# Latent attention of a two-block transformer kernel: one written order per engine over eleven lines of work, four banks in one ring

## The chip, the cores and the metric

The kernel runs on one core of one Trainium2 chip. The metric is the device time of one execution in microseconds (us), lower is better. Of the kernel before, three runs are shown: 2634.11, 2634.42 and 2637.79 us.

## What is computed

Two transformer blocks follow each other on 512 tokens of width 1024. The first (dilated attention with retention, cross attention, a gated MLP) is untouched here. The second has a gated delta-rule branch and a latent-attention branch over the same tokens and 256 context tokens, a merge of the two by gates, and an MLP. The change lies between the end of the delta rule and the merge, and that stage computes:

```python
q = (_rms(cq, q_a_norm) @ w_uq).reshape(B, T, 8, 192)
kv = (_rms(ckv, kv_a_norm) @ w_ukv).reshape(B, T, 8, 256)
k_nope, v = kv[..., :128], kv[..., 128:]
k = concatenate([k_nope, broadcast(k_rope)])
q, k = _rms(q, q_norm), _rms(k, k_norm)        # then rotary on the last 64
s = einsum('bqhd,bkhd->bhqk', q, k) * 192 ** -0.5
o = softmax(s) @ v                             # 512 queries, 768 keys
y = _rms(o_gdn, w_norm) * silu(z)              # the delta rule's output, gated
```

cq, ckv, k_rope and z are projections of the normed tokens (ckv and k_rope of the context too).

## The kernel before

Everything is held with channels on partitions. Large projections are made from weight chunks of 128 x 1024, streamed by SyncE's DMAs into raw slots (three in turn in this stage). ACT writes the rounded chunk (`hi_to`), DVE the remainder (`lo_to`), and `project` makes three rounded products for each of eight input tiles: 24 products of 128 x 512 for a chunk. Attention itself is in exact f32.

Each engine runs one instruction queue in order. Between engines there are semaphores by name: `up` counts an event, `at` waits for it, `fence` for several. A PSUM bank may be written again when the events in `free[bank]` have come. The functions are generators: each `yield` ends a turn, and the order in which a driver calls the generators of an engine is the order of its queue.

The latent stage has these parts, each with one generator per engine it uses:

- **Ranks** (`rank_pe`, `rank_act`, `rank_dve`): cq by three chunks, ckv by two, k_rope by one; sums of squares by a product with ones, root, scaling. They run whole, before all else.
- **Front of a head** (`front_pe`, L2257, and its ACT, DVE and POOL parts): queries from cq (on even heads a second product for the rotary parts of two heads), keys and values from ckv; squares by ACT, the rotary part's squares added by POOL, sums by TensorE, roots by ACT, scaling by DVE. The squares of queries and of both key groups (512 and 256 tokens) share two buffers in turn, `SQM`, L2168.
- **Attention of a head** (`latent_pe`, L2417): four blocks of 128 queries. A score block is four products into a pair of banks, 2 and 3 or 4 and 5 in turn; DVE takes the row maximum, ACT the exponential with its sum, DVE scales by the reciprocal, TensorE transposes six squares of 128 into two banks, DVE copies the four of the first and ACT the two of the second. After the fourth block the six value products run. `attend_turns2`, L2412, is the written order of the 12 turns within a head.
- **Gates and norm** (`z_pe`, L2111, and others): eight projections of z with a Silu each, then for eight groups the norm of the delta rule's output (POOL squares, DVE sums, ACT root, DVE scaling), a transposition and the multiplication with the gate.

`latent_step`, L2506, puts these together on every engine: in step h it calls in turn the attention of head h-1, the front of head h and four turns of the gates and norm, one turn each, until all are at their end. `weave` is that round-robin:

```python
for step in range(9):
    latent_step(step, lambda h: latent_pe(e, h), lambda h: front_pe(e, h, take), zg)

def latent_step(step, attend, front, zg):
    weave(*(([attend(step - 1)] if step else []) + ([front(step)] if step < 8 else []) + [some(zg, 4)]))
```

So steps 0 to 3 hold two gate projections each, steps 4 to 7 two groups of norm turns. TensorE's front and gates take banks 0 and 1 in turn (`take`, L2530), the transposes and the values 6 and 7. A Silu and an exponential are in different ACT table sets, and a switch is an extra instruction (L140). SyncE (`latent_sp`, L2509) loads w_uq, w_uk and w_uv head by head into one place each, so each load waits for the products of the head before; the gate chunks stand between them, and the first merge chunks behind all. The delta-rule stage before this one already takes its order from strings, one letter per turn (`walk_streams`, L2029).

Lines that the rows name are those of helpers: L130 product, L133 transpose, L142 activation, L143 exponential with sum, L140 table load, L146 copy, L155 tensor-tensor, L160 tensor-scalar, L163 scalar-tensor-tensor, L172 row reduction.

Of the kernel before, what the change touches and what calls it, by code (L numbers as in the profile page):

```python
# [16 lines left out]
KT = 8  # L17
# [186 lines left out]
def program(nc, D, out):  # L204
    tally = Tally()
    at, up, land = tally.at, tally.up, tally.land
    with ExitStack() as ctx:
# [1821 lines left out]
        def walk_streams(engine, streams):  # L2029

            for x in TURNS[engine]:
                next(streams[x], None)
            for g in streams.values():
                whole(g)
# [6 lines left out]
        def gdn_pe(e):  # L2041
# [6 lines left out]
            walk_streams("PE", dict(  # L2048
# [4 lines left out]
        def gdn_act(e, got):  # L2053
            fence(e, mlp_end)
            walk_streams("ACT", dict(
# [4 lines left out]
        def gdn_dve(e, got):  # L2060
            walk_streams("DVE", dict(
# [4 lines left out]
        def gdn_pool(e):  # L2066
            fence(e, mlp_end)
            walk_streams("POOL", dict(
# [18 lines left out]
        KR2, SQR = hcT, hcT + 768  # L2087
# [12 lines left out]
        chunks[first_merge + 5]["after"] = [("l_uq", 7), ("l_uk", 7)]  # L2100

        def z_turns():
            for mt in range(8):
                yield "z", mt, 0
                yield "z", mt, 1
            for blk in range(4):
                for g in range(2):
                    yield "norm", blk, g
                    yield "turn", blk, g

        def z_pe(e, take):  # L2111
            for what, i, g in z_turns():
                if what == "z" and g == 0:
                    b = take()
                    whole(project(e, CI["w_z", i], KT, [(b, NT, *HX, hx)]))
                    free[b], BK["z", i] = [("z_ev", i)], b
                elif what == "turn":
                    b = take()
                    fence(e, [("z_on", i, g)] + free[b])
                    for j in range(4):  # L2120
                        t = e.transpose(P(b * 512 + j * 128, 128), S(OS + i * 1024 + g * 512 + j * 128, 128), IDN)
                    t.then_inc(*up("z_tr", i, g))
                    free[b], BK["z_tr", i, g] = [("z_y", i, g)], b
                yield

        def z_act(e, got):
            for what, i, g in z_turns():
                if what == "z" and g == 0:
                    hi_to(e, got, min(CI["w_z", i][0] + 1, last_two))
                    e.wait_ge(*at("w_used", CI["w_z", i][0]))  # L2130
                    e.act(S(y1 + i * NT, NT), P(BK["z", i] * 512, NT), ACT.Silu).then_inc(*up("z_ev", i))
                elif what == "norm":
                    e.wait_ge(*at("z_red", i, g))
                    e.act(S(ST8 + 8, 4), S(ST8, 4), ACT.Ln, scale=1.0 / 128, bias=S(EPS6, 1)).then_inc(*up("z_ln", i, g))
                    e.wait_ge(*at("z_ln", i, g))
                    e.act(S(ST8 + 16, 4), S(ST8 + 8, 4), ACT.Exp, scale=-0.5).then_inc(*up("z_rs", i, g))
                yield

        def z_dve(e, got):
            for what, i, g in z_turns():  # L2140
                og = OS + i * 1024 + g * 512
                if what == "z" and g == 0:
                    lo_to(e, got, min(CI["w_z", i][0] + 1, last_two))
                elif what == "norm":
# [11 lines left out]
        def z_pool(e, before):  # L2156
            for what, i, g in z_turns():
                if what == "norm":
                    if i or g:
                        e.wait_ge(*at("z_red", i - 1 + g, 1 - g))  # L2160
# [37 lines left out]
        def rank_act(e, got):  # L2198
# [4 lines left out]
            for k in range(3):  # L2203
                square_of(e, k, cqT + k * NT, NT, [("cq_ev", k)])
# [803 lines left out]
```

## Time and profile before

| | before |
|---|---|
| median of three runs | 2634.42 us |
| the profiled execution's own time | 2637.32 us |
| span of its trace | 2635.5 us |
| TensorE busy, whole span | 2431.4 us, 92% |
| DVE, ACT, POOL busy | 48%, 37%, 10% |
| mean granted TensorE clock | 0.961 |

A window's row gives for a stretch of the trace the busy time of each engine; the granted clock is a share of 2.4 GHz. A timeline merges neighbouring instructions of one line, shows where the run starts, how long it is, and in brackets how long the engine had been idle and which engine's work ended the wait. PEld is TensorE's weight load, which overlaps its products. An exact-f32 product appears as two records. "issue" in the chain of waits is time in which the view sees no wait.

### The profile page before, as it was taken

To read this page: it belongs to the slowest core of one execution; us is meant where nothing else is said; L and a number is where in the kernel's file an instruction comes from. 1 tells how busy PE (TensorE), PEld (TensorE's weight loads), DVE (VectorE), ACT (ScalarE), POOL (GpSimd) and SP (SyncE) were. 2 spreads that over 40 slices of the span, in tenths; PEclk is the share of its full clock that TensorE was granted. 3 is DMA by queue.
4 is the path that set the end of the run, shared out by engine and by line. 5 is a ranking of instruction groups with operands and counts; after the bars stand their busy time and mean duration, and the time that the engine had idled before them with its cause. 6 is when DMAs were issued, how large, how long until landed. Compare 5 with 4: busy or idle time off the path is not lost.

```text
span 2635.5 us, 29341 instructions
## 1 busy us (share of the span) xinstructions
PE 2431.4 (92%) x11836; PEld 1922.5 (73%) x11836; DVE 1267.7 (48%) x1976; ACT 962.1 (37%) x1684; POOL 272.5 (10%) x289
## 2 busy tenths in 40 slices
PE   6999787898999998899999999989988899899999
PEld 3676676565877876688888888866655588688887
DVE  3343445326645633665677777323344443543442
ACT  3234234333222222543544445344433432342331
POOL 0000010013000010021233323000011000100000
PEclk9999999998999996899999999999999899899999
DMA  4211122113545521101000001111001033233332
GB/s 156 80 56 49 56 88 88 48 56 120 191 128 184 186 78 61 45 29 53 33 25 25 19 23 41 41 63 48 14 16 49 24 124 128 72 96 97 97 101 81
DMA packets 60038, 195.70 MB, mean 74 GB/s; under 512 B 6656, under 2 KB 11520, under 8 KB 59520
## 3 DMA queue, kind: packets, MB, share of 16 engines
q1 hardware_dynamic: 59904, 193.83, 21.9%
q8 instruction: 95, 1.56, 0.2%
q14 instruction: 39, 0.32, 0.0%
HBM read 187.25 MB, written 6.55 MB: 74 GB/s over the span
## 4 chain that ended last, share of the span: by engine, by line
PE 80%; DVE 11%; ACT 5%; issue 2%; POOL 2%; DMA 0%; SPq 0%; DVEq 0%; ACTq 0%; POOLq 0%
PE ps L130 76%; PE ps L133 4%; DVE r L155 3%; DVE sb L155 2%; DVE sb L163 2%; ACT sb L142 2%; DVE sb L160 1%; ACT r L142 1%; DVE sb L172 1%; ACT sb L143 1%; POOL sb L155 1%; POOL sb L146 1%; ACT L140 0%; DVE sb L146 0%; POOL sb L160 0%
## 5 line engine op out<-in xcount | busy, mean ns | idle before, releaser
L130 PE MATMUL ps<-r 128*128 128x512 f32 (+1 forms) x7032 | 1619.0, 389 | 70.1 <-DVE r L155 58.8
L130 PEld LDWEIGHTS ps<-r 128*128 128x128 f32 x7032 | 1286.0, 191 | 370.8 <-DVE r L155 66.6
L130 PE MATMUL ps<-sb 128*128 128x128 f32 (+5 forms) x3806 | 760.5, 347 | 79.7 <-ACT sb L142 52.8
L130 PEld LDWEIGHTS ps<-sb 128*128 128x128 f32 (+1 forms) x3806 | 543.4, 200 | 257.8 <-issue 128.6
L155 DVE TENSOR_TENSOR r<-sb,r 128x1024 fp32r<-128x1024 f32 (+3 forms) x437 | 451.5, 1040 | 523.4 <-ACT r L142 522.6
L142 ACT ACTIVATE r<-sb 128x1024 fp32r<-128x1024 f32 (+3 forms) x437 | 375.7, 879 | 535.3 <-PE ps L130 304.0
L142 ACT ACTIVATE sb<-ps 128x512 f32<-128x512 f32 (+3 forms) x556 | 251.8, 470 | 679.7 <-PE ps L130 520.3
L155 POOL TENSOR_TENSOR sb<-sb 128x512 f32<-128x512 f32 (+3 forms) x173 | 194.6, 1129 | 1813.3 <-ACT sb L142 1200.7
L163 DVE SCALAR_TENSOR_TENSOR sb<-sb 128x512 f32<-128x512 f32 (+5 forms) x240 | 231.2, 974 | 84.6 <-ACT sb L142 82.4
L155 DVE TENSOR_TENSOR sb<-ps,sb 128x256 f32<-128x256 f32 (+1 forms) x252 | 147.8, 596 | 244.4 <-PE ps L130 237.3
L133 PE MATMUL ps<-sb 128*128 128x128 f32 (+1 forms) x998 | 151.3, 282 | 51.1 <-DVE sb L146 17.6
L142 ACT ACTIVATE sb<-sb 128x512 f32<-128x512 f32 (+5 forms) x286 | 143.6, 519 | 110.2 <-DVE sb L181 28.2
L155 DVE TENSOR_TENSOR sb<-sb 128x512 f32<-128x512 f32 (+2 forms) x166 | 131.7, 794 | 91.6 <-ACT sb L142 88.0
L133 PEld LDWEIGHTS ps<-sb 128*128 128x128 f32 (+1 forms) x998 | 114.3, 144 | 80.8 <-DVE sb L160 42.1
L142 ACT ACTIVATE sb<-ps,sb 128x128 f32<-128x128 f32 (+2 forms) x181 | 82.6, 465 | 129.6 <-PE ps L130 129.4
L163 DVE SCALAR_TENSOR_TENSOR sb<-ps,sb 128x128 f32<-128x128 f32 (+1 forms) x224 | 80.6, 403 | 94.5 <-PE ps L130 93.4
L140 ACT ACT_TABLE_LOAD x63 | 80.8, 1283 | 73.1 <-PE ps L130 40.7
L155 DVE TENSOR_TENSOR sb<-sb,ps 128x256 f32<-128x256 f32 (+2 forms) x128 | 61.9, 484 | 74.5 <-PE ps L130 73.7
L172 DVE TENSOR_REDUCE sb<-ps 128x1 f32<-128x768 f32 (+1 forms) x48 | 37.2, 776 | 106.4 <-PE ps L130 106.4
L160 DVE TENSOR_SCALAR sb<-sb 128x1 f32<-128x1 f32 (+5 forms) x144 | 68.0, 476 | 13.6 <-ACT sb L142 10.2
L160 POOL TENSOR_SCALAR sb<-sb 128x128 f32<-128x128 f32 x80 | 55.4, 700 | 169.2 <-PE ps L130 102.0
L143 ACT ACTIVATE sb<-ps,sb 128x768 f32<-128x768 f32 (+1 forms) x48 | 39.3, 820 | 80.7 <-DVE sb L160 63.9
(23 smaller groups left out, 172.0 us busy)
## 6 DMA issues: line engine op xcount, KB each, us to landing
sb<-in_w_mlp SPq DMA_DIRECT2D x64, 512.0 KB, 3.5
sb<-in_w_mod SPq DMA_DIRECT2D x48, 512.0 KB, 4.4
sb<-in_w_qkv SPq DMA_DIRECT2D x24, 512.0 KB, 3.3
sb<-in_w_g SPq DMA_DIRECT2D x22, 512.0 KB, 3.3
sb<-in_w_u SPq DMA_DIRECT2D x22, 512.0 KB, 3.3
sb<-in_w_out SPq DMA_DIRECT2D x16, 512.0 KB, 3.4
sb<-in_w_down SPq DMA_DIRECT2D x16, 512.0 KB, 3.5
sb<-in_w_gate SPq DMA_DIRECT2D x16, 512.0 KB, 3.3
```

The lines of the kernel that those rows point to most:

```text
L130: return QUIET if self.e is None else self.e.matmul(o, l, r, start=start, stop=stop)
L133: return QUIET if self.e is None else self.e.transpose(o, i, ident)
L140: self.e.preload_act_table_set(self.set)
L142: return self.e.activation(o, i, f, bias=bias, scale=scale)
L143: return self.e.activation(o, i, f, bias=bias, scale=scale, accum_out=acc)
L146: return QUIET if self.e is None else self.e.tensor_copy(o, i)
L155: return QUIET if self.e is None else self.e.tensor_tensor(o, a, b, op)
L160: return self.e.tensor_scalar(o, a, s1, None, op0) if op1 is None else self.e.tensor_scalar(o, a, s1, s2, op0, op1)
L163: return QUIET if self.e is None else self.e.scalar_tensor_tensor(o, a, s, b, op0, op1)
L172: return QUIET if self.e is None else self.e.tensor_reduce(o, i, AX.X, op, negate=negate)
```

## The change

`front` and `latent` are split into lines of work: ranks (on DVE two, the scaling of ckv apart), queries, keys, values up, scores, values (transposes and value products), gates, norm, and on ACT and DVE one each for the weight chunks: eleven. A line of queries, keys, values up, scores or values runs over all eight heads. Each engine has a string in `TURNS2`, one letter per turn, and `walk_streams` follows it. `project` ends a turn after half of each piece. Norm groups are taken in another order, the first half of the heads for all blocks first, so that the last four gate projections may come late.

All of TensorE's takes but the scores go round banks 0, 1, 6 and 7. Scores keep their two pairs. The squares of the queries get their own buffer, `SQQ`, and the two key groups one buffer each. The keys' two groups signal apart. Gate chunks are loaded one for each head in place of two, w_uk's load waits for the second key group. No product, activation or vector operation is added or left out.

```diff
+        TURNS2 = {
+            "PE": ("kkkkkkkkkkkkkkkkkkzkkzkkkzzffzffzqquutfftffzzqquunqtffvvttvffvvvtvvtvvvvvtvvzvvzvqquuntfftffzzqquutf"
+                "fvvttvffvvvtvvzvzqqqtvvtffvvtffvvvtvqvvvvvttqvvuvvttqunnvvvtffvvtffvvzzvvzqquuntvfftfffqqtvvvvtvvttv"
+                "vqquutvvvvvtvvtuuuvvnnvvnn"),
+            "DVE": ("wnnnwnwwkkkkkkkwwwKKwKkkffqwffttnvnntvvvwttvvvffvvttvvvvtvvvqnnnwffttvvtvvwtvvvffvttvqvvttvvvvvffttv"
+                "vvtvvtvvvttvvnnnnvwntnvvtffvvvqqnnnttvvftvfvvtfvvvttvvtwvvvwwttvvvvnnnnnn"),
+            "ACT": ("wnkwnkwkkkwkkkkwkkwkkkkwkkkzkkkwzffffzqquuffwffzqqtuqnuttwvfftffvvtvttvvvvtvzvqquunffwffzqqtuuttvwff"
+                "tffvvvvzqqttqvttffvffvvqttvvvttqvuvquttnwvvntffvffvtzvzqquunvfffqffttqvtvvtvqqtuuttwvvwvwvttuuuvnnvv"),
+            "POOL": ("nnnffqffqnffqnffqffqffqnnffqnnfffqq"),
+        }
+
+        def walk_streams(table, engine, streams):
+
+            for x in table[engine]:
                 next(streams[x], None)
...
-        KR2, SQR = hcT, hcT + 768
+        KR2, SQR, SQQ = hcT, hcT + 768, hcT + 1280
...
+        GATE_LOADS = (2, 3, 4, 5, 6, 7, 7, 7)
+        GATE_TURNS = [(0, 0), (1, 0), (2, 0), (3, 0), (0, 1), (1, 1), (2, 1), (3, 1)]
...
+        def gate_pe(e, take):
+            for i in range(8):
+                b = take()
+                yield from project(e, CI["w_z", i], KT, [(b, NT, *HX, hx)], 4)
+                free[b], BK["z", i] = [("z_ev", i)], b
+                yield
...
+        def norm_pe(e, take):
+            for i, g in GATE_TURNS:
+                b = take()
+                fence(e, [("z_on", i, g), ("z_ev", 4 * g + 3)] + free[b])
+                for j in range(4):
...
         def rank_pe(e, take):
             for mt in range(3):
                 b = take()
-                whole(project(e, CI["w_cq", mt], KT, [(b, NT, *HX, hx)]))
+                yield from project(e, CI["w_cq", mt], KT, [(b, NT, *HX, hx)], 4)
                 free[b], BK["cq", mt] = [("cq_ev", mt)], b
+                yield
             b = take()
...
+            if h:
+                e.wait_ge(*at("l_sum", "q", h - 1))
+            e.act(S(SQQ, NT), P(BK["q", h] * 512, NT), ACT.Square).then_inc(*up("l_sq", "q", h))
...
+        def key_pe(e, h, take):
+            for g, (n0, n) in enumerate(TOK):
+                b = take()
+                fence(e, [("uk", h)] + free[b])
+                for k in range(2):
+                    e.wait_ge(*at("ck_n", k))
+                    m = e.matmul(P(b * 512, n), S(WUK + k * 128, 128), S(ckT + k * NA + n0, n), k == 0, k == 1)
+                m.then_inc(*up("l_uk", h, g))
+                free[b], BK["k", h, g] = [("l_sq", "k", h, g)], b
+                yield
+            for g, (n0, n) in enumerate(TOK):
+                b = take()
+                fence(e, [("l_add", "k", h, g)] + free[b])
+                e.matmul(P(b * 512, n), ONES, S(SQM[g], n), True, True).then_inc(*up("l_sum", "k", h, g))
+                free[b], BK["k_sum", h, g] = [("k_ln", h, g)], b
+                yield
...
+        def key_act(e, h):
+            kh = KH[h % 2]
+            for g, (n0, n) in enumerate(TOK):
+                e.wait_ge(*at("l_uk", h, g))
+                if h >= 2:
+                    e.wait_ge(*at("s_s", h - 2, 3))
+                e.act(S(kh + n0, n), P(BK["k", h, g] * 512, n), ACT.Copy, scale=sm("k_norm", 0)).then_inc(*up("k_ev", h, g))
+                e.wait_ge(*(at("l_sum", "k", h - 1, g) if h else at("l_sum", 6)))
+                e.act(S(SQM[g], n), P(BK["k", h, g] * 512, n), ACT.Square).then_inc(*up("l_sq", "k", h, g))
...
+        def score_pe(e, h):
+            qh, qr, kh = QH[h % 2], QR[h // 2 % 2], KH[h % 2]
+            for new in range(4):
+                u = 4 * h + new
+                b = 2 + 2 * (u % 2)
+                fence(e, [("lq_rot", h - h % 2), ("q_ev", h), ("k_n", h, 1)] + free[b] + free[b + 1])
+                for n0, n in TOK:
+                    e.matmul(P(b * 512 + n0, n), S(qh + new * 128, 128), S(kh + n0, n), True, False)
+                    m = e.matmul(P(b * 512 + n0, n), S(qr + new * 128, 128), S(kh + NA + n0, n), False, True)
+                m.then_inc(*up("s_s", h, new))
+                free[b] = free[b + 1] = [("s_e", u)]
+                yield
...
+        def score_act(e, h):
+            for new in range(4):
+                u = 4 * h + new
+                st = STM[u % 6]
+                e.wait_ge(*at("s_b", u))
+                if u >= 3:
+                    e.wait_ge(*at("s_t", u - 3, 1))
+                e.act(S(SCM[u % 3], NA), P((2 + 2 * (u % 2)) * 512, NA), ACT.Exp, scale=S(RQ[h % 2] + new, 1),
+                      bias=S(st + 3, 1), acc=S(st + 1, 1)).then_inc(*up("s_e", u))
+                yield
...
+        def value_pe(e, h, take):
+            for old in range(4):
+                u = 4 * h + old
+                for g, (b0, nb) in enumerate(((0, 4), (4, 2))):
+                    b = take()
+                    fence(e, [("s_v", u)] + free[b])
+                    for j in range(nb):
+                        t = e.transpose(P(b * 512 + j * 128, 128), S(SCM[u % 3] + (b0 + j) * 128, 128), IDN)
+                    t.then_inc(*up("s_t", u, g))
+                    free[b], BK["pt", u, g] = [("pt_a" if g else "pt_d", h, old)], b
                     yield
...
-                    e.wait_ge(*at("l_uk", h - 1))
+                    e.wait_ge(*at("l_uk", h - 1, 1))
...
-                load_to(e, got, min(CI["w_z", 0][0] + 2 * h + 3, last_two))
+                load_to(e, got, min(CI["w_z", 0][0] + GATE_LOADS[h], last_two))
...
         def latent_pe_all(e):
             count = [0]
 
             def take():
                 count[0] += 1
-                return (count[0] - 1) % 2
-
-            rank_pe(e, take)
-            zg = z_pe(e, take)
-            for step in range(9):
-                latent_step(step, lambda h: latent_pe(e, h), lambda h: front_pe(e, h, take), zg)
-            whole(zg)
+                return (0, 1, 6, 7)[(count[0] - 1) % 4]
+
+            walk_streams(TURNS2, "PE", dict(
+                k=rank_pe(e, take), q=over(range(8), lambda h: query_pe(e, h, take)),
+                f=over(range(8), lambda h: key_pe(e, h, take)), u=over(range(8), lambda h: up_pe(e, h, take)),
+                t=over(range(8), lambda h: score_pe(e, h)), v=over(range(8), lambda h: value_pe(e, h, take)),
+                z=gate_pe(e, take), n=norm_pe(e, take)))
 
         def latent_act_all(e, got):
             fence(e, gdn_end)
-            rank_act(e, got)
```

## Rows read from the trace of the kernel before

**Rows 1.** The page's first part, busy us (share of the span) and instructions of each engine.
```profile
PE 2431.4 (92%) x11836; PEld 1922.5 (73%) x11836; DVE 1267.7 (48%) x1976; ACT 962.1 (37%) x1684; POOL 272.5 (10%) x289
```

**Rows 2.** Windows: us, busy of PE, PEld, DVE, ACT, POOL, granted clock, DMA share, GB/s.
```profile
1696.10:2090.90 394.80, 348.81 (x1425) 231.68 (x1424) 151.85 (x253) 156.06 (x296) 37.49 (x32) 0.97 0.10 34
1812.50:1857.30 44.80, 42.08 (x173) 27.81 (x173) 17.78 (x29) 21.37 (x37) 3.69 (x3) 1.00 0.11 34
1857.30:1899.40 42.10, 39.48 (x166) 26.59 (x167) 13.58 (x23) 19.69 (x35) 4.31 (x4) 1.00 0.05 16
1899.40:1941.70 42.30, 35.56 (x132) 22.02 (x132) 18.40 (x33) 14.04 (x33) 6.22 (x5) 0.92 0.04 11
1941.70:1977.10 35.40, 31.17 (x126) 19.73 (x126) 16.39 (x28) 13.46 (x32) 5.59 (x5) 0.95 0.06 20
```

**Rows 3.** Timeline of TensorE's weight loads in an unbroken exact-f32 run: start, us, idle before.
```profile
1946.40 0.19 PEld L130 LDWEIGHTS ps<-sb 128*128 128x128 f32 x1 [0.24 <-issue]
1946.83 0.19 PEld L130 LDWEIGHTS ps<-sb 128*128 128x128 f32 x1 [0.24 <-issue]
```

**Rows 4.** Chain of waits, in order of time: start us, us, what.
```profile
1792.33 0.65 PE ps L133 x6
...
1937.82 0.97 DVE sb L172
1938.82 0.23 DVE sb L160
1939.09 0.87 issue
1940.38 0.62 DVE sb L160
1941.00 0.61 DVE sb L146
```

**Rows 5.** Timeline of TensorE: start us, us, operation, idle before and releaser.
```profile
1696.13 16.58 PE L130 MATMUL ps<-r 128*128 128x512 f32 x72
...
1726.08 8.55 PE L130 MATMUL ps<-r 128*128 128x512 f32 x48 [0.78 <-ACT sb L142]
...
1745.44 1.98 PE L130 MATMUL ps<-sb 128*128 128x512 f32 x4 [1.48 <-ACT sb L142]
1749.17 6.28 PE L130 MATMUL ps<-sb 128*128 128x256 f32 x16 [1.75 <-ACT sb L142]
...
1812.57 0.84 PE L133 MATMUL ps<-sb 128*128 128x128 f32 x6 [2.01 <-DVE sb L146]
...
1922.08 1.31 PE L133 MATMUL ps<-sb 128*128 128x128 f32 x10 [2.03 <-DVE sb L155]
1923.23 3.53 PE L130 MATMUL ps<-sb 128*128 128x512 f32 x16
...
1930.79 7.00 PE L130 MATMUL ps<-sb 128*128 128x512 f32 x16 [1.17 <-ACT sb L142]
...
2008.51 5.40 PE L130 MATMUL ps<-sb 128*128 128x512 f32 x16 [1.17 <-ACT sb L142]
```

**Rows 6.** Timeline of ACT at a table load, end of the stage.
```profile
2097.04 1.28 ACT L140 ACT_TABLE_LOAD   x1 [4.95 <-PE ps L130]
2098.33 0.60 ACT L142 ACTIVATE sb<-ps 128x512 f32<-128x512 f32 x1
```

**Rows 7.** DMA issues: count, KB each, median us to landing.
```profile
sb<-in_w_z SPq DMA_DIRECT2D x8, 512.0 KB, 3.3
...
sb<-in_w_uk SPq DMA_DIRECT2D x8, 128.0 KB, 2.0
```

**Rows 8.** Groups by form in 1696.1 to 2090.9, rounding of weights and their remainder.
```profile
L155 DVE TENSOR_TENSOR r<-sb,r 128x1024 fp32r<-128x1024 f32 x15 | 20.2, 1351 | 35.5 <-ACT r L142 35.5
...
L142 ACT ACTIVATE r<-sb 128x1024 fp32r<-128x1024 f32 x15 | 15.7, 1056 | 1.1 <-DVE sb L155 1.1
```

**Rows 9.** Who waited for whom in 1737 to 2104: us in total, times, longest.
```profile
PE ps L133 <- DVE sb L146: 17.6, 9, 2.8
```

More of the change, by code:

```diff
@@ L2099, in program @@
         chunks[first_merge + 3]["after"] = chunks[first_merge + 4]["after"] = [("w_used", CI["w_kr", 0][0])]
[L2100 to L2123, printed above, removed]
-                yield
@@ L2126, in z_act @@
[L2126 to L2136, printed above, removed]
-                yield
@@ L2139, in z_dve, with hi_act @@
[L2139 to L2144, printed above, removed]
+        chunks[first_merge + 5]["after"] = [("l_uq", 7), ("l_uk", 7, 1)]
+        GATE_LOADS = (2, 3, 4, 5, 6, 7, 7, 7)
+        GATE_TURNS = [(0, 0), (1, 0), (2, 0), (3, 0), (0, 1), (1, 1), (2, 1), (3, 1)]
+        def hi_act(e, got):
+            while got[0] <= first_merge + 1:
+                hi_to(e, got, got[0])
+                yield
@@ L2168, in square_of, with norm_pool @@
-        def square_of(e, i, o, n, events, bank=None):
-            fence(e, events)
+                    yield
+        def norm_pool(e, before):
+            for k, (i, g) in enumerate(GATE_TURNS):
+                if k:
+                    e.wait_ge(*at("z_red", *GATE_TURNS[k - 1]))
+                og = OS + i * 1024 + g * 512
+                e.wait_ge(*at(*before[0]))
+                e.tt(S(ZSQ, 512), S(og, 512), S(og, 512), MU).then_inc(*up("z_sq", i, g))
+                before[0] = ("z_sq", i, g)
+                yield
@@ L2234, in rank_dve @@
                 e.stt(S(cqT + k * NT, NT), S(cqT + k * NT, NT), sm("q_a", k), S(RL, NT), MU, MU).then_inc(*up("cq_n", k))
-            for mt in range(3):
-                lo_to(e, got, (CI["w_ckv", mt][0] if mt < 2 else CI["w_kr", 0][0]) + 1)
+                yield
             e.wait_ge(*at("c3_in"))
@@ L2450, in latent_dve @@
[L2450 to L2461 removed]
+                e.tt(k, k, S(KR2 + n0, n, n=64), AD).then_inc(*up("l_add", "k", h, g))
@@ new lines, in key_pool, with up_pe @@
+                before[0] = ("l_add", "k", h, g)
+                yield
+        def up_pe(e, h, take):
+            for g, (b0, nb) in enumerate(((0, 4), (4, 2))):
+                b = take()
+                fence(e, [("uv", h)] + free[b])
+                for j in range(nb):
+                    for k in range(2):
+                        e.wait_ge(*at("ck_n", k))
+                        m = e.matmul(P(b * 512 + j * 128, 128), S(ckT + k * NA + (b0 + j) * 128, 128), S(WUV + k * 128, 128),
+                                     k == 0, k == 1)
+                m.then_inc(*up("l_uv", h, g))
+                free[b], BK["v", h, g] = [("v_ev", h, g)], b
+                yield
@@ L2562, in latent_pool @@
             before = [("c_kd", 7, 1, 4)]
-            zg = z_pool(e, before)
-            for h in range(8):
-                weave(front_pool(e, h, before), some(zg, 4))
-            whole(zg)
+            walk_streams(TURNS2, "POOL", dict(
+                q=over(range(8), lambda h: query_pool(e, h, before)), f=over(range(8), lambda h: key_pool(e, h, before)),
+                n=norm_pool(e, before)))
         mL = OS
```

390 lines of the change are left out of this document (164 added, 226 removed).

## The prediction

> **What bounds the kernel now.** I read the page first: TensorE is busy 92% of the span, no other engine half of it [rows 1]. So time can only come from where TensorE waits or runs slowly, and the change touches one stage. I cut that stage out with windows [rows 2]: from TensorE's first product of the latent stage (1696.1) to its first product of the merge (2090.9) it takes 394.8 us, of which TensorE is busy 348.8, so it idles 46.0 us. ACT (156 us) and DVE (152 us) are at two fifths, POOL at a tenth: none is a bound.
>
> Busy time is not work, so I built the work from undisturbed rows. In exact f32 a 128x512 product is two records, and weight loads in an unbroken run of them start 0.43 us apart [rows 3], so such a product costs 0.86, a 256-wide one 0.43, a 128-wide one 0.215. Six transposes follow each other in 0.65 [rows 4]: 0.108 each. A rounded product costs 16.58/72 = 0.230, and a w_ckv or w_kr chunk (24 of 512, 24 of 256) 8.55 [rows 5].
> - Ranks: 16.6 (cq) + 3 x 8.55 + sums of squares 2.6 + 2.6 = 47.5.
> - Eight gate projections of 24 rounded products: 8 x 5.52 = 44.2.
> - A head: queries 2.58 (twice that on even heads, mean 3.87), their one-column sums 0.96 (the 3.53 of a block of 16 [rows 5] less a score's 2.58), keys 2.58, key sums 1.29, values up 2.58, four scores 4 x 2.58 = 10.3, 24 transposes 2.6, values 5.16: 29.4; times 8 = 235.
> - Norm transposes 32 x 0.108 = 3.5.
>
> Together 330 us. Against 394.8 that leaves 65 us: 46 idle and 19 of stretched records. The steps check this. The two steps with gate projections and full clock take 44.8 and 42.1 for 41.7 and 39.1 of work, and their busy time is only 1% above the work; the two after them, with norms for filler, take 42.3 and 35.4 for 31.5 and 28.9 of work, at a granted clock of 0.92 and 0.95 [rows 2]. The excess lies where the filler is thin.
>
> What TensorE waits for is in its timeline [rows 5]: 1.48 and 1.75 in the rank stage for squares from ACT, 0.78 for a bank of the ring of two, 2.01 for a copy by DVE once in every head, 2.03 for the normalised rows of the norm. The chain of waits shows why: after a score, the row maximum 0.97, its scaling 0.23, then 0.87 until the exponential and its sum are through, the scaling of the row 0.62, a copy 0.61 [rows 4]. That is 3.3 us from the end of a score to the end of the copy that frees the transposes' bank, and the fixed round-robin puts work of its own choosing, not enough work, between.
>
> **The change, part by part.** No arithmetic is added or removed; only order, banks and one buffer.
>
> *The order.* I spelled out the four strings, turn by turn, and followed TensorE's with the durations above. Rank stage: half of gate projection 0 (2.76) now stands between w_kr and its squares' sums, which covers the 1.48, and the other half between the sums of the two token groups, which covers the 1.75: 3.2 us. From there the question is whether the work between a score and the transposes of the same score exceeds the 3.2 us that the maximum, exponential and scaling take. The tightest places: score 1.3 has two transposes' groups and half a gate projection behind it, 0.65 + 2.76 = 3.4; score 7.3 has transposes 0.65 and head 7's values up 2.58 = 3.2; score 4.3 has 4.9; score 6.3 has two further scores, 5.8. Between the last transposes of a head and its value product stand a score, a gate half, a query sum or two norm groups (0.86, in the last head), against a copy of 0.7. The score of head 3's third block needs the first block's exponential, which needs the query roots; behind the query sum stand queries 4 (5.16), against two table loads of 1.28 [rows 6] and a few short activations. By this walk hardly any wait is longer than a few tenths, so the 46 us of idle go almost whole. I don't take that at face value: it has no slack in five or six places, and an in-order queue passes each delay on. I charge 10 us of new waits (about 0.3 us at each of 32 score units) and keep 2 us of rank waits that stay (the squares of cq follow its last projection as before).
>
> *The stretch.* The 19 us are mostly half clock: the same block of 16 products, behind the same 1.17 of idle, takes 5.40 in one head and 7.00 in another [rows 5], and the granted clock is lowest in the steps with the most idle [rows 2]. With the gaps gone I let the stretch fall to the 1% of the two dense steps, 4 us; its ends are 0 and the old 19. The Trainium skill, "TensorE: Matmul & The Clock Gate", part on the clock gate, says that the throttled clock is the default and that sustained activity releases it; the trace agrees in direction, and by the rule alone the 4 us would be 0.
>
> *The ring of four banks (0, 1, 6, 7).* Before, the front's products went round 0 and 1 and transposes round 6 and 7. It removes the 0.78 waits, two of them (1.6 us). What it adds: every product now waits for the reader of the fourth take before it, whichever engine that is. Queued behind such a wait on TensorE is everything. Where I looked the reader is an ACT or DVE evictor within its own stretch; the closest is the third transposes of head 0, about 0.5 us late. That is in the 10.
>
> *Own buffer for query squares.* Queries no longer share the two square buffers with the keys, so keys of the next head can be squared before the query sum is through. Instructions: none more. It costs nothing, and its gain is part of the order.
>
> *SyncE's queue.* Keys of head h+1 now come before queries of h+1, but their weights are still loaded behind w_uq's, which waits for the queries of head h. On TensorE at least 5.1 us of work (values up and one score, heads 1 and 4) stand between; two issues and a landing of 2.0 [rows 7] are about 3. Hidden; without that cover it would be up to 3 us a head. Gate chunks are loaded one per head, three slots deep, landing in 3.3 [rows 7], well before use. The first merge chunks are queued behind values-up of head 6, which now comes late; from there to the merge's first product lie 20 us of TensorE work, against 3.3 for the load and 1.06 + 1.35 for rounding and remainder [rows 8]. Hidden too.
>
> *Table loads.* Eight Silus still fall among exponentials, so the number of switches stays at some 16. A load takes 1.28 and the next activation starts at its end, 2097.04 to 2098.33 [rows 6]. The Trainium skill, "ScalarE: Activation LUTs", section on what ACT_TABLE_LOAD costs, gives about 2.66 us with the drain; this trace doesn't show the drain. By that figure the loads ahead of the eight query roots would each add 1.38 to a place with no slack: an estimate of 11 us, from that page, and a time of some 2596. The sum goes by the row.
>
> *The end.* The merge's start (gates, roundings of both branches) keeps its order behind the same events, so it moves as a block.
>
> **Sum.** 330 + 4 + 2 + 10 = 346 us in place of 394.8: 49 us less. That is against the profiled execution, 2637.3 (span 2635.5), 3 us above the median of the three runs shown, 2634.4; I take the 49 from the median, since a difference of 3 us is as likely to lie elsewhere: **2585**.
>
> **Rivals.**
> *B, half the gaps survive.* The strings presuppose durations; where ACT or DVE stand at a turn whose input is late, all turns behind it are late, and the ring carries it to TensorE. If half of idle and stretch stay (33 us), the stage takes 363 and the kernel 2603; with more, 2612. For it: five tight places, and each engine's queue strictly in order. Against it: ACT and DVE are free for half the time.
> *C, slower.* Each unit's transposes wait as one group per head does today, 2.01 us for a DVE copy or scaling that stands behind a maximum on DVE's queue. At 32 units that is 64 us, and with such gaps the stretch stays at 19: 330 + 19 + 2 + 64 = 415, 20 us more than now, kernel **2655**; the gain is gone when the mean wait per unit passes (65 - 21)/32 = 1.4 us. Against it: DVE is idle for 60% of the stage. It would need a systematic misordering, and following the DVE string I found maximum, scaling and copy of neighbouring units alternating.
> *D, it doesn't do what it says.* Letters of a string beyond the end of their line of work are skipped and any leftover is run at the end; if a line's turns are off by one, work bunches at the end, and the time stays within 0.2% of before. The strings' counts match the turns but for a few superfluous letters, so this is remote.
>
> **How the numbers follow.** Forecast (A) 0.80, B 0.13, C 0.04, D 0.03. Lower end: all idle and stretch go but the 2 us, 332, kernel 2571. Upper end: into B, 2606. That leaves out the rest of B, C and D. A and B are faster by over 0.2% (5 us, about what a measurement of this kernel can tell from no change): 0.93; D is same, 0.03; C slower, 0.04.
>
> **What would show it.** Right: from the first rank product to the first merge product 346 us within 15; TensorE idle there under 20 us; the waits of transposes for the DVE copy, 17.6 us now (9 times) [rows 9], under 5; granted clock at 0.98 or more; idle of ACT and DVE smaller since their busy time hardly changes. The waits at w_ckv of 0.78 and those of 1.48 and 1.75 are gone. Wrong: a recurring wait of over 1 us per score unit, a wait of keys' products for w_uk (SyncE late), or TensorE waiting for merge weights; and any movement outside the stage, which I hold at zero.

## The result and the profile after

| | before | changed |
|---|---|---|
| median, us | 2636.11 (4 runs, 2634.11 to 2638.81) | 2574.74 (4 runs, 2571.85 to 2577.56) |
| ratio | | 0.9766, 95% interval 0.9750 to 0.9783 |
| span of the profiled execution | 2635.5 | 2573.3 |

The changed kernel is 61.4 us faster, 2.3%. The forecast was 49 us less; the time lies in the range, near its fast end. The stage gives 62.0 us. Outside it two small shares nearly cancel: the changed kernel's profiled execution enters the stage 1.5 us later and is 1.7 us shorter behind it (both are taken up below). These are the windows of the changed kernel, with the columns of [rows 2]: the stage whole, then in five parts, then the start of the merge.

```profile
1697.60:2030.40 332.80, 330.88 (x1425) 224.48 (x1424) 151.65 (x252) 157.86 (x299) 37.12 (x32) 1.00 0.12 41
1697.60:1765.00 67.40, 66.20 (x311) 52.97 (x311) 21.66 (x30) 30.18 (x47) 5.69 (x5) 1.00 0.20 65
1765.00:1832.00 67.00, 66.91 (x288) 44.67 (x287) 33.34 (x56) 35.25 (x68) 7.95 (x7) 1.00 0.11 33
1832.00:1900.00 68.00, 68.00 (x269) 43.00 (x268) 23.82 (x39) 33.89 (x61) 7.95 (x7) 1.00 0.10 32
1900.00:1965.00 65.00, 65.00 (x278) 42.57 (x278) 40.64 (x71) 29.64 (x66) 9.13 (x8) 1.00 0.07 24
1965.00:2030.40 65.40, 64.78 (x286) 41.28 (x284) 32.19 (x57) 28.90 (x60) 6.40 (x5) 1.00 0.14 50
2030.40:2044.90 14.50, 11.19 (x52) 8.94 (x49) 6.88 (x11) 9.10 (x16) 0.00 (x0) 1.00 0.38 108
```

The stage takes 332.8 us where it took 394.8 [rows 2]. TensorE is idle for 1.9 us of it (46.0 before) and its busy time fell from 348.8 to 330.9 with the same 1425 records: the clock is granted in full in every part. DVE and ACT do what they did, 152 and 158 us (151.9 and 156.1 before; ACT has 17 table loads where it had 15). So 44 us came from idle and 18 from stretched records.

TensorE's timeline, which answers to [rows 5]:

```profile
1697.61 16.59 PE L130 MATMUL ps<-r 128*128 128x512 f32 x72
1715.40 3.10 PE L130 MATMUL ps<-sb 128*128 128x512 f32 x6 [1.20 <-ACT sb L142]
1717.95 28.33 PE L130 MATMUL ps<-r 128*128 128x512 f32 x156
1746.11 1.88 PE L130 MATMUL ps<-sb 128*128 128x512 f32 x4
1747.43 3.33 PE L130 MATMUL ps<-r 128*128 128x512 f32 x12
...
1813.57 7.89 PE L130 MATMUL ps<-sb 128*128 128x512 f32 x20
1821.30 1.47 PE L133 MATMUL ps<-sb 128*128 128x128 f32 x12
...
1825.77 3.01 PE L130 MATMUL ps<-r 128*128 128x512 f32 x12
1828.63 1.04 PE L133 MATMUL ps<-sb 128*128 128x128 f32 x6
1829.42 3.00 PE L130 MATMUL ps<-r 128*128 128x512 f32 x12
...
2023.31 1.72 PE L133 MATMUL ps<-sb 128*128 128x128 f32 x14 [0.62 <-DVE sb L146]
2024.87 5.33 PE L130 MATMUL ps<-sb 128*128 128x512 f32 x12
...
2030.39 11.17 PE L130 MATMUL ps<-r 128*128 128x512 f32 x48
2044.87 5.73 PE L130 MATMUL ps<-r 128*128 128x512 f32 x24 [3.31 <-DVE r L155]
```

The two waits of 0.78 are gone: the ckv and k_rope chunks and half of gate projection 0 are one run of 156 records from 1717.95. The sums of squares at 1746.11 wait for nothing, and a gate half follows at 1747.43. At 1825.77 and 1829.42 the halves of gate projection 4 stand around the last transposes of head 1, the place where I had counted 3.4 us of cover against 3.2. In the whole stage two waits are left, 1.20 for the squares of cq and 0.62 for the last transposes. The 0.62 is a wait for a bank, not for the score. The row scaling of the last unit ends at 2022.56, but the bank that its transposes take is freed only by DVE's copy for the unit before, and this stands behind that scaling in DVE's queue:

```profile
2022.48 0.68 DVE L146 COPY sb<-ps 128x512 f32<-128x512 f32 x1
```

Behind the stage the wait at the start of the merge is as before, 3.31 us; this one was not touched. What follows it is shorter. These are the 8.3 us behind this wait in the kernel before, in the changed kernel and in a second profile of the changed kernel (its run is described below):

```profile
2105.68:2114.00 8.32, 8.32 (x25) 6.57 (x25) 5.89 (x9) 3.95 (x7) 0.00 (x0) 0.65 0.00 0
2044.87:2053.20 8.33, 8.11 (x34) 6.39 (x35) 7.72 (x11) 5.01 (x8) 0.00 (x0) 1.00 0.15 45
2043.17:2051.50 8.33, 8.33 (x30) 6.78 (x31) 6.59 (x10) 5.00 (x8) 0.00 (x0) 0.82 0.04 4
```

After the same 3.3 us of idle the granted clock was 0.65, 1.00 and 0.82, so 25, 34 and 30 products fit. Nine more of 0.23 us are 2 us, so the 1.7 us lie here. The last two rows are of the same kernel: this share varies from execution to execution.

Who waited for whom in 1680 to 2045 (the stage and some 15 us on either side), us in total, times, longest:

```profile
ACT sb L142 <- PE ps L130: 102.8, 51, 7.5
...
PE ps L133 <- DVE sb L146: 0.6, 1, 0.6
```

The second row was 17.6 us in nine waits [rows 9]; it is 0.6 in one. The engines that wait are the others. TensorE is their bound now.

### The profile page after: what moved, and what is told of

It is laid out like the page before. It is cut to its first block, busy times and chain, and to the rows that moved or that the text cites. A ratio compares the mean times of both kernels' runs of the same rounds, so it can differ in the third digit from the quotient of the medians.

```text
span 2573.3 us, 29372 instructions
## 1 busy us (share of the span) xinstructions
PE 2411.1 (94%) x11836; PEld 1913.7 (74%) x11836; DVE 1267.9 (49%) x1976; ACT 963.0 (37%) x1686; POOL 271.8 (11%) x289
## 4 chain that ended last, share of the span: by engine, by line
PE 83%; DVE 9%; ACT 4%; POOL 2%; issue 2%; DMA 0%; SPq 0%; DVEq 0%; ACTq 0%; POOLq 0%
PE ps L130 79%; PE ps L133 4%; DVE r L155 3%; DVE sb L163 2%; DVE sb L155 2%; ACT sb L142 2%; ACT r L142 1%; DVE sb L160 1%; POOL sb L155 1%; POOL sb L146 1%; ACT sb L143 0%; ACT L140 0%; POOL sb L160 0%; DMA sb<-in_w_aq 0%; DVE sb L172 0%
## 5 line engine op out<-in xcount | busy, mean ns | idle before, releaser
L130 PE MATMUL ps<-sb 128*128 128x128 f32 (+5 forms) x3806 | 749.4, 344 | 69.2 <-ACT sb L142 44.9
L130 PEld LDWEIGHTS ps<-sb 128*128 128x128 f32 (+1 forms) x3806 | 536.4, 198 | 239.7 <-issue 119.3
L133 PEld LDWEIGHTS ps<-sb 128*128 128x128 f32 (+1 forms) x998 | 113.6, 142 | 49.9 <-DVE sb L160 20.0
L142 ACT ACTIVATE sb<-ps,sb 128x128 f32<-128x128 f32 (+3 forms) x181 | 82.5, 465 | 139.8 <-PE ps L130 139.6
L160 DVE TENSOR_SCALAR sb<-sb 128x768 f32<-128x768 f32 (+5 forms) x144 | 69.9, 489 | 49.1 <-ACT sb L142 45.8
L146 DVE COPY sb<-ps 128x512 f32<-128x512 f32 (+5 forms) x76 | 38.0, 511 | 24.7 <-PE ps L133 21.5
```

The costliest lines, as they stand in the source:

```text
L130: return QUIET if self.e is None else self.e.matmul(o, l, r, start=start, stop=stop)
L133: return QUIET if self.e is None else self.e.transpose(o, i, ident)
L142: return self.e.activation(o, i, f, bias=bias, scale=scale)
L146: return QUIET if self.e is None else self.e.tensor_copy(o, i)
L160: return self.e.tensor_scalar(o, a, s1, None, op0) if op1 is None else self.e.tensor_scalar(o, a, s1, s2, op0, op1)
```

## The experiments

Twelve more runs were made beside the kernel before; one is the changed kernel again, and the kernel with the merge's edit was run twice. "Stage" is always the stretch from the first rank product to the first merge product in that kernel's profile.

### The new banks and buffers with the old order

```diff
 # latent_pe, on the kernel before (its readers on DVE and ACT take the bank from a table)
-                    b = 6 + (9 * h + 2 * old + g) % 2
+                    b = take()
...
 # latent_pe_all
-                return (count[0] - 1) % 2
+                return (0, 1, 6, 7)[(count[0] - 1) % 4]
```

> The kernel before with one edit: all takes but the scores' go round banks 0, 1, 6, 7, the order of every engine as before. Theory (the order is the gain, the ring only makes it possible): the two waits of 0.78 us at the w_ckv and w_kr chunks go, the stage from the first rank product to the first merge product falls from 394.8 to about 393, idle from 46 to about 44, and the time is within 3 us of before. Rival (the rings of two held TensorE back): 10 to 30 us faster, with the recurring wait of 2.01 us for DVE's copy gone from every head.

Measured: 2634.95 us against 2636.1, ratio 0.9996 (0.9987 to 1.0005). And with the queries' squares in their own buffer on top:

```diff
...
+            if h:
+                e.wait_ge(*at("l_sum", i0 - 3))
+            e.act(S(SQQ, NT), P(BK["q", h] * 512, NT), ACT.Square).then_inc(*up("l_sq", i0))
...
+                e.wait_ge(*at("l_sum", i0 - 2 + g if h else 6))
+                e.act(S(SQM[g], n), P(BK["k", h][g] * 512, n), ACT.Square).then_inc(*up("l_sq", i0 + 1 + g))
```

> As the run before, and the queries' squares in a buffer of their own, each key group its own buffer; so the new kernel's banks and buffers with the old order. Theory: nothing more than the ring alone, within 2 us of it, since in the old order the query sum stands ahead of the keys anyway; all but 2 us of the 62 us lie in the order. Rival: the shared buffers held ACT's squares back, 5 us or more less than with the ring alone.

Measured: 2635.25, ratio 0.9997 (0.9988 to 1.0006). The stage's window in the first and then in the second:

```profile
1693.95:2088.17 394.22, 349.65 (x1424) 232.63 (x1424) 151.81 (x253) 156.00 (x296) 37.49 (x32) 0.96 0.10 35
```

```profile
1695.42:2089.52 394.10, 349.52 (x1424) 232.62 (x1424) 151.81 (x253) 156.00 (x296) 37.49 (x32) 0.96 0.10 35
```

Of the 62 us, banks and buffers alone give 0.7. In idle the ring gives 1.4 us (46.0 to 44.6, about the two waits of 0.78), and the own buffer nothing (44.6 again); the stretch rose by 0.8. TensorE's timeline of the first still has the waits of the old order, once in each head the 2.01 and in the norm steps the 1.55:

```profile
1807.85 0.84 PE L133 MATMUL ps<-sb 128*128 128x128 f32 x6 [2.01 <-DVE sb L146]
...
1854.19 0.85 PE L133 MATMUL ps<-sb 128*128 128x128 f32 x6 [2.01 <-DVE sb L146]
...
1925.21 1.31 PE L133 MATMUL ps<-sb 128*128 128x128 f32 x10 [1.55 <-DVE sb L155]
```

So the gain lies in what is left: the order, and the small things that belong to it (halved projections, the order of the norm groups, the keys' two signals, the order of the loads). As written it does need more banks than before: between the halves of gate projection 2 (`zffz` in TensorE's string) come the two sums of the first head's keys. In the old front ring of two the second of them would take the bank in which the gate projection is half done. The halves of gate projection 4 would not need it; what stands between them are transposes, and these had banks 6 and 7. An order with fewer banks was not run. Nor was the order itself taken apart: whether its gain comes more from scores of the next head ahead of a value product, from keys two heads ahead or from halved gate projections stays open, except for the one half tried below.

### The term of the rank stage

```diff
-            "PE": ("kkkkkkkkkkkkkkkkkkzkkzkkkzz
+            "PE": ("kkkkkkkkkkkkkkkkkkkkzkkzkzz
```

> The new kernel with one edit in TensorE's string: the sums of squares of the first token group follow directly on w_kr, then the two halves of gate projection 0 split the sums of the second group, so that no gate half stands between w_kr and its squares. Theory (a term of 3.2 us in my sum): a wait like the 1.48 us of before comes back behind w_kr, idle of the stage 1.9 to about 3.5 to 5, the time 1.5 to 4 us more. Rival (later turns absorb it, since something else ends the stage): no more than 1 us.

Measured: 2575.33 us (2574.62 to 2575.89) against 2574.74. Window of the stage and the row of TensorE's timeline:

```profile
1695.31:2030.26 334.95, 331.56 (x1424) 224.30 (x1424) 152.72 (x252) 157.85 (x299) 37.28 (x32) 1.00 0.12 41
```

```profile
1742.71 1.99 PE L130 MATMUL ps<-sb 128*128 128x512 f32 x4 [1.48 <-ACT sb L142]
```

The wait of 1.48 is back and the stage is 2.1 us longer (334.95): 1.5 of idle and 0.7 of stretch. The wait of 1.75 doesn't come back, since a gate half still stands before the sums of the second group. The times of whole runs don't resolve the 2.1. The term is right in kind: nothing later absorbed it.

### How much slack the order has

A second row maximum ahead of each of the 32, written to a spare column:

```diff
                 e.wait_ge(*at("s_v", u - 6))
+                e.reduce(S(BGT + 818, 1), P((2 + 2 * (u % 2)) * 512, NA), MAX, negate=True)
                 e.reduce(S(st, 1), P((2 + 2 * (u % 2)) * 512, NA), MAX, negate=True)
```

> The new kernel with a second row maximum over the same 768 scores ahead of each of the 32, into a spare column: 0.95 us more on DVE in the chain from score to exponential, 30 us in all. Theory 1 (there is slack between score and transposes in nearly every unit, and I was wrong to charge 10 us for five or six places without any): 0 to 3 us more. Theory 2 (as I wrote: the tight places have none): each of the five or six places, and what is behind them in order, pays 0.95 or more, 5 to 10 us. Theory 3 (DVE bounds): 30 us.

Three more, in columns 817, 818 and 819:

> The same with three more maxima per unit, 2.86 us in the chain, 91 us of DVE in all (DVE then 243 of 333 us). If the typical cover beyond the chain's 3.2 us is about 2 to 4 us, this breaks it at the tight places only: 10 to 25 us more. If the cover is typically below 1 us (theory 2), 60 us and more. The difference between this run and the one with one maximum tells how the slack is spread.

One more in the kernel before:

> The kernel before with the same one extra maximum per unit. If the chain from score to transposes was what ended TensorE's waits there, as rows 4 and 5 are read, about three of four units in each head pay the whole 0.95: 20 to 28 us more, where the new kernel pays hardly anything. If the old waits came from something else (banks, squares), it pays little as well, under 8 us.

And a small one in the changed kernel, a scaling of one column:

```diff
+                e.ts(S(BGT + 818, 1), S(st, 1), S(RQ[h % 2] + new, 1), MU)
                 e.ts(S(st + 3, 1), S(st, 1), S(RQ[h % 2] + new, 1), MU)
```

> The new kernel with one more scaling of a 128x1 column (0.21 us) in each of the 32 chains from score to exponential. The run with 0.95 us more had 8 us more of stage in seven new waits of 0.7 to 1.5 us. If those places had no slack at all, 0.21 us more each gives 1.5 to 2 us; if they have some tenths, nothing.

| kernel | added per unit, us | time, us | stage, us | idle, us |
|---|---|---|---|---|
| changed | 0 | 2574.74, 2573.85 | 332.8 | 1.9 |
| changed, small | 0.21 | 2573.23 | 333.4 | 2.2 |
| changed, one maximum | 0.95 | 2580.55 | 340.8 | 8.3 |
| changed, three maxima | 2.86 | 2630.01 | 389.3 | 38.8 |
| before | 0 | 2636.11 | 394.8 | 46.0 |
| before, one maximum | 0.95 | 2664.43 | 428.9 (slowest of four executions) | 62.8 |

The windows of the stage, one maximum in the changed kernel, three in it, one in the kernel before:

```profile
1695.91:2036.71 340.80, 332.49 (x1424) 224.06 (x1424) 177.00 (x284) 157.70 (x299) 36.97 (x32) 1.00 0.12 40
```

```profile
1695.80:2085.05 389.25, 350.42 (x1425) 231.18 (x1424) 231.34 (x348) 156.74 (x299) 36.95 (x32) 0.96 0.11 35
```

```profile
1697.70:2126.55 428.85, 366.04 (x1424) 244.76 (x1424) 178.57 (x285) 155.23 (x296) 37.46 (x32) 0.92 0.09 32
```

In the kernel before, 0.95 us in the chain of each unit costs 27.7 us (2664.43 against 2636.77 beside it, forecast 20 to 28). The profiled execution was the slowest of its four, 2673.03 us where the other three took 2663.9 to 2664.9, and nearly all its difference to the profile of the kernel before lies in the stage. So its 34 us of stage are probably some 8 more than usual, and can't be set against the 30.4 us that were added. Of the 34, 16.8 are idle and 17.2 are stretched records (busy time 366.0 against 348.8, at a clock of 0.92). Not every unit pays: 16.8 us are 19 waits made longer by 0.87. In the steps with gate projections two waits grow, in the later ones three or four. The two are the 0.64 before the second keys' sum, now 1.50, and the 2.01 before the transposes, now 2.88:

```profile
1855.41 3.71 PE L130 MATMUL ps<-sb 128*128 128x256 f32 x12 [1.50 <-ACT sb L142]
...
1863.94 1.49 PE L133 MATMUL ps<-sb 128*128 128x128 f32 x6 [2.88 <-DVE sb L146]
```

So the chain of the score was exposed in the old order, at two to four places in a head. In the changed kernel the same work costs 5.8 us of time and 8.0 of stage. Its new waits are these, from TensorE's timeline (two more are of 0.2):

```profile
1808.86 0.85 PE L133 MATMUL ps<-sb 128*128 128x128 f32 x6 [0.90 <-DVE sb L146]
...
1828.70 1.04 PE L133 MATMUL ps<-sb 128*128 128x128 f32 x6 [0.74 <-DVE sb L160]
...
1913.09 1.56 PE L130 MATMUL ps<-sb 128*128 128x512 f32 x4 [1.23 <-POOL sb L155]
...
1937.45 0.84 PE L133 MATMUL ps<-sb 128*128 128x128 f32 x6 [1.38 <-ACT sb L142]
...
2002.06 0.88 PE L133 MATMUL ps<-sb 128*128 128x128 f32 x6 [0.82 <-DVE sb L160]
...
2029.62 1.72 PE L133 MATMUL ps<-sb 128*128 128x128 f32 x14 [1.49 <-DVE sb L146]
```

They are few, and four of the six stand where the prediction's walk had put them: 1808.86 is the third transposes of head 0, 1828.70, 1937.45 and 2029.62 are the transposes of scores 1.3, 4.3 and 7.3. The other two were not on its list.

The small addition of 0.21 us shows only two waits, 0.16 at the third transposes of head 0 and 0.74 where 0.62 was, but the stage grew by 0.6. The rest hides in gaps too short for the timeline to show as waits. At score 1.3 the half gate projection and the transposes behind it now start 2.98 us apart, where it was 2.86 (1825.77 and 1828.63 above):

```profile
1822.12 2.98 PE L130 MATMUL ps<-r 128*128 128x512 f32 x12
1825.10 1.04 PE L133 MATMUL ps<-sb 128*128 128x128 f32 x6
```

Lined up by their starts with the second profile of the changed kernel, the small run falls behind by 0.15, 0.12, 0.09 and 0.08 us at the first four of the six places and by 0.11 at the last. So by this estimate (0.21 less what was lost) the first four have 0.06 to 0.13 us of slack, the last has none, and nearly everywhere else there is more than 0.21.

Theory 1 of the first run is out (0 to 3 us); 5.8 is inside the 5 to 10 of theory 2, and the tight places have a tenth or less in place of the "none" it says. The run with three maxima cost 55 us (56.5 of stage: 36.9 of idle and 19.6 of stretch), near the upper of its two cases (10 to 25 with a cover of 2 to 4 us, 60 and more with under 1). The added idle is 1.15 us for each unit against 2.86 added; by this estimate the order covers on average 1.7 us more than the chain needs. With 2.86 the gain is almost gone.

### Table loads

This kernel leaves out the gate's nonlinearity, and with it the switches of table set:

```diff
-                e.act(S(y1 + i * NT, NT), P(BK["z", i] * 512, NT), ACT.Silu).then_inc(*up("z_ev", i))
+                e.act(S(y1 + i * NT, NT), P(BK["z", i] * 512, NT), ACT.Copy).then_inc(*up("z_ev", i))
```

> The new kernel with a copy in place of Silu on z (the gate's nonlinearity is left out), so that ACT has no table switches in the stage: 16 loads of 1.28 us less. By the row of the load and the idle of 1.9 us: no change of the time beyond 1 us, since ACT is covered. If a switch really cost about 2.66 us ahead of each of the query roots and this were in TensorE's path, up to 10 us less. The trace also shows how ACT's idle and its activations around a switch stand without the load.

One run: 2572.93 us. The stage:

```profile
1694.65:2027.44 332.79, 330.87 (x1424) 224.54 (x1424) 152.25 (x252) 137.79 (x283) 36.56 (x32) 1.00 0.12 41
```

332.8 us again, to the hundredth, with ACT busy 137.8 in place of 157.9. The 20.1 us that went are about the 16 loads (20.5 by their rows of 1.28). The table loads cost this order nothing. Nor is there time lost around one where activations stand on both sides of it, as in the changed kernel here:

```profile
1752.08 0.60 ACT L142 ACTIVATE sb<-ps 128x512 f32<-128x512 f32 x1
1752.70 1.28 ACT L140 ACT_TABLE_LOAD   x1
1753.99 0.47 ACT L142 ACTIVATE sb<-ps,sb 128x256 f32<-128x256 f32 x1
```

### The merge's start

```diff
                     hi_to(e, got, CI["w_gate", 8 * g + mt][0] + 1)
+                    if mt == 0:
+                        for k in range(KT):
+                            e.act(R(hi + k * NT, NT), S(lo + k * NT, NT), ACT.Copy).then_inc(*up(ev + "_hi", k))
                     e.wait_ge(*at("w_used", CI["w_gate", 8 * g + mt][0]))
```

> The new kernel with one edit at the start of the merge: ACT rounds the eight tiles of each branch before it waits for the gate projection's end and takes the sigmoid, not after. The profile of the new kernel has 3.31 us of TensorE idle there, ended by DVE's remainders, which wait for ACT's rounding. Theory: the roundings start some 6 us earlier and the 3.31 goes, 3 us less (2571.5 against 2574.7), hardly more than a measurement tells. Rival: the wait moves to the gates (sigmoids come later and the multiplications by the gates with them), no change.

Measured: 2567.94 us (2567.16 to 2570.52, 5 runs), ratio 0.9742 (0.9729 to 0.9755). That is 6.8 below the first runs of the changed kernel, more than the wait is long, so both were run again side by side:

> The new kernel unchanged, beside the one with the merge's roundings first, on the same chip: 2574 to 2577 us. It gives the base for the other three and shows how far the part before the stage, which is the same code, moves by itself.

> The same edit as f4, run beside the new kernel. If the 6.8 us between f4 and the first runs of the new kernel are all the edit's, 7 us less than the run beside it. If part of it came from the stretch before the stage, 3.5 to 5 us less, which is what the windows from the stage's end to the end of the kernel give (542.9 against 538.0).

Measured: 2573.85 (2573.03 to 2574.81) and 2568.40 (2567.00 to 2569.29), 5.4 apart and the runs don't overlap. TensorE's timeline at the merge in the first and in the second:

```profile
2028.71 11.15 PE L130 MATMUL ps<-r 128*128 128x512 f32 x48
2043.17 97.18 PE L130 MATMUL ps<-r 128*128 128x512 f32 x416 [3.30 <-DVE r L155]
```

```profile
2028.50 111.78 PE L130 MATMUL ps<-r 128*128 128x512 f32 x487
```

The gates' 48 products and the first branch are one unbroken run (487 records to the end of the view at 2140); the 3.30 is gone. From the first merge product to the end of the span it is 543.9 (2572.6 less 2028.71) and 539.0 (2567.5 less 2028.50), 4.9 less. Of these, 3.3 are this wait, and 1.4 are the stretch behind it: the granted clock was 0.82 in the 8.3 us after the wait (the third of the three windows in the section on the result), and is 1.00 from the first merge product to 2198 with the edit. This is the fastest kernel of the study. The same edit in the kernel before:

> The kernel before with the merge's roundings first. The wait of 3.30 us at its merge's start is the same as in the new kernel and lies behind the stage, so it should give the same 3.5 to 5 us as there: the two edits add. If the gain depended on the new order, under 1 us.

Measured: 2632.13 against 2635.18, ratio 0.9983 (0.9974 to 0.9993): 3 us, a little less than forecast, with an interval that takes in 1.8 to 6.9. The profiles say more. First the merge's first 746 records in the kernel before and in this one, then this one's stage:

```profile
2090.88:2267.47 176.59, 173.29 (x746) 141.41 (x745) 73.72 (x85) 57.87 (x79) 10.86 (x6) 0.98 0.35 118
```

```profile
2093.47:2263.66 170.19, 170.19 (x746) 139.49 (x745) 73.78 (x85) 57.92 (x79) 10.87 (x6) 1.00 0.38 122
1695.77:2093.47 397.70, 353.46 (x1425) 234.00 (x1424) 151.77 (x253) 155.85 (x296) 37.47 (x32) 0.95 0.10 34
```

In the merge the edit is worth 6.4 us here: the wait of 3.30 and 3.1 of stretch, with the clock of 0.65 behind the wait. The stage, with the same instructions as before, took 397.7 us in this profile where it took 394.8. So the edit works in either order and is not tied to the new one. Each number is one profile's, and the stage of the old order varies by about 3 us.

## Why the prediction was right, and by how much it was off

*The work.* 330 us was the figure that carried the sum, and it holds: with 1.9 us of idle the stage takes 332.8, so its records take 330.9.

*The cause.* That the round-robin left too little between a score and its transposes is shown by the extra maximum, which costs 28 us before and 6 after, and by the old order, which keeps the old time with the new banks. Not all of the 46 us of idle was this: the copy ends 17.6 us of waits [rows 9], and the timelines show others for the norm's rows, for ACT's squares and for the first query sum. They went with the same change, and no run separates them.

*The ring and the buffer.* I gave the ring 1.6 us and the buffer nothing; the idle fell by 1.4 and by nothing. In the stage the two together gave 0.7, less than the 3 us by which it varies, and neither can be told from no change in the time. The ring's own price was named too (each product waits for the reader of the fourth take before it): such a wait is the 0.62 at the last transposes, though the old pair of banks 6 and 7 would have made them wait for the same copy.

*The term that was mis-sized: new waits.* I charged 10 us, 0.3 at each score unit, because I saw "no slack in five or six places" and took it that each delay is passed on. New waits were 0.6 us. My walk with the durations of the rows had found hardly any, and hardly any came; what failed is the discount on it. That makes 9.4 of the 13.2 us between the forecast stage of 346 and the measured 332.8; 3.1 are the stretch and 0.8 the rank waits. The durations that the walk rests on stayed where they were (the maximum's mean is 955 ns before and 952 after, the exponential's 992 in both; the largest move I saw is the row scaling, 621 to 680), and the order repeats itself: four profiles with this order unchanged in the stage give 332.76 to 332.80.

But the margin was smaller than the walk knew. It had 0.2 us to spare at score 1.3 and called the third transposes of head 0 half a microsecond late; the small run puts their slack at 0.09 and 0.06. That both came out without a wait is in part luck: the walk isn't exact to a tenth.

*A chain that was summed wrong.* "3.3 us from the end of a score to the end of the copy" leaves out the reciprocal and the handovers. The rows that it is taken from run from 1937.82 to 1941.61 [rows 4], 3.8. The 3.2 that the walk compares with is right: from the start of the maximum to the end of the row scaling, 1941.00, it is 3.2.

*The stretch.* 4 us kept, under 1 measured (330.9 against 330). At a granted clock of 1.00 throughout there is no half clock to pay, and the 19 us fell with the idle. The rule that sustained activity releases the clock (the Trainium skill, "TensorE: Matmul & The Clock Gate", section "What's actually happening"), which I had weighed against the row, would have given this 0; the trace agrees with it within the 0.9. The runs show how idle and stretch go together in the same stage, with about 330 us of work in each:

| kernel | idle, us | stretch over 330, us | granted clock |
|---|---|---|---|
| changed | 1.9 | 0.9 | 1.00 |
| changed, one maximum | 8.3 | 2.5 | 1.00 |
| changed, three maxima | 38.8 | 20.4 | 0.96 |
| before, merge's roundings first | 44.2 | 23.5 | 0.95 |
| before | 46.0 | 18.8 | 0.97 |
| before, one maximum | 62.8 | 36.0 | 0.92 |

The stretch is 0.3 to 0.6 of the idle, but the amount of idle doesn't fix it: the fourth and fifth rows have the same instructions in the stage and differ by 5 us.

*The rank waits.* 2 us kept, 1.2 stayed. Of the 3.2 us of the two gate halves the run without the first half tests one term: it is 2.1 us of stage for the wait of 1.48.

*Table loads.* Against the 2.66 us with a drain (the Trainium skill, "ScalarE: Activation LUTs", section "What ACT_TABLE_LOAD costs") this case's rows decide for 1.28: a load starts 0.02 us after one activation ends, and the next starts at its end. Without loads the stage is the same, so the alternative of 2596 is out. The number of loads in the stage was not kept at "some 16" but rose from 15 to 17.

*SyncE.* No wait of TensorE for w_uk or for merge weights is in the timeline. The covers of 5.1 and 20 us held.

*The rivals.* B (half the gaps stay, stage 363) is out: 1.9 us of 46 stayed. It lies between what 0.95 and 2.86 us more per unit do, 341 and 389. C needed a mean wait of 1.4 us per unit; the mean is 0.02. D is excluded by the timeline, which has the halves where the strings put them.

## What to carry to other kernels

Work out the bounding engine's pure work for a stage from undisturbed rows of its own trace; where it is well under the stage's time and no other engine is near it, the order can be worth that difference, in idle and in half clock together. To see whether a written order will hold, walk it with measured durations and compare, for each dependent pair, the work between against the chain's length; where single durations were as steady as here, the walk was nearer the truth than the walk with a discount. To see how close an order is to breaking, add a known piece to the chain and count the new waits; compare starts too, since delays of a tenth don't show as waits.

## What was not expected

The stretch before the stage, the same code in all kernels, ended between 1693.8 and 1697.7 us in the profiled executions: the changed kernel entered the stage 1.5 us later than the kernel before and the f and g kernels up to 2.3 earlier. Differences of 3 us between whole runs can't be put down to an edit without the windows; the merge's edit looked like 6.8 us against one set of runs and was 4.9 in the windows. The window has to be the right execution's, too: the extra maximum in the kernel before looked like 34 us in the profile of its slowest execution and is 28 by the median.

An added 0.95 us per unit cost more than itself in the kernel before (34.1 against 30.4 us of stage), since the idle it made lowered the clock from 0.97 to 0.92.
